# Alternating ScalarE's output copies with gate banks in slot 20 of a two-layer GLA and retention trunk

## The reference

```python
h = _rmsnorm(x, norm_w)
z = jnp.einsum('btd,dc->btc', h, w_in).astype(F32)
gq, gk, gv, gg, glr, rq, rk, rv, rg = _split_cols(z)
...
o_a = o_a * lax.rsqrt(jnp.mean(o_a * o_a, axis=-1, keepdims=True) + EPS) * gla_norm_w.astype(F32)
o_a = o_a.reshape(B, T, GLA_WIDTH) * jax.nn.silu(gg)
mu = jnp.mean(o_b, axis=-1, keepdims=True)
var = jnp.mean(jnp.square(o_b - mu), axis=-1, keepdims=True)
o_b = ((o_b - mu) * lax.rsqrt(var + GN_EPS)).reshape(B, T, RET_WIDTH)
o_b = (o_b * ret_norm_w.astype(F32) + ret_norm_b.astype(F32)) * jax.nn.silu(rg)
mixed = jnp.concatenate([o_a, o_b], axis=-1).astype(x.dtype)
y = x + jnp.einsum('btc,cd->btd', mixed, w_out)
```

## Time and profile before

| | us |
|---|---|
| median of 3 runs | 1630.08 |
| lowest, highest | 1627.74, 1633.01 |
| the profiled execution's own time | 1630.65 |
| its span (first to last instruction) | 1628.8 |
| PE busy | 1598.0 (98%) |
| DVE busy | 1116.3 (69%) |
| ACT busy | 641.2 (39%) |
| POOL busy | 839.1 (52%) |
| mean granted TensorE clock | 0.996 of full |

### The profile page before, as it was taken

One profiled execution on the slowest core, in us unless ns is written; L12 is line 12 of the kernel. 1 busy time (PEld: TensorE's weight loads), 2 busy tenths in 40 slices (PEclk: granted clock), 3 DMA queues, 4 the chain that ended last, 5 costly groups with the idle time before them and its releaser, 6 DMA issues.

```text
span 1628.8 us, 30453 instructions
## 1 busy us (share of the span) xinstructions
PE 1598.0 (98%) x11840; PEld 1303.4 (80%) x11840; DVE 1116.3 (69%) x2402; ACT 641.2 (39%) x1184; POOL 839.1 (52%) x646
## 2 busy tenths in 40 slices
PE   9998999989999999999999999999999999999998
PEld 7787878878888887888778888787788887878887
DVE  5955876768765585557855477758887567784684
ACT  5423434334343443434443344343433435343342
POOL 4543645646455464455544455456544455554465
PEclk9999999999999999999999999999999999999999
DMA  8356656766445564466643676576764466553654
GB/s 287 114 97 166 200 202 162 215 180 207 173 118 156 168 197 137 122 169 154 203 136 100 160 162 191 162 194 188 184 189 134 126 166 163 173 170 92 168 160 144
DMA packets 389296, 268.32 MB, mean 165 GB/s; under 512 B 290720, under 2 KB 293280, under 8 KB 389152
## 3 DMA queue, kind: packets, MB, share of 16 engines
q1 hardware_dynamic: 315280, 131.86, 31.8%
q10 hardware_dynamic: 73872, 134.51, 26.1%
HBM read 219.21 MB, written 47.07 MB: 163 GB/s over the span
## 4 chain that ended last, share of the span: by engine, by line
PE 78%; DVE 11%; DMA 4%; SPq 3%; issue 2%; ACT 1%; POOL 0%; ACTq 0%; POOLq 0%; DVEq 0%
PE bank L785 70%; DVE region L1582 3%; PE bank L1032 2%; PE bank L994 2%; PE bank L1043 1%; SPq L486 1%; DMA out_o_rows<-region 1%; SPq L472 1%; DVE bns L1559 1%; DVE tmp L1599 1%; PE bank L751 1%; PE bank L1017 1%; DVE m_lo L1615 1%; PE bank L879 1%; DMA out_k_rows<-region 1%
## 5 line engine op out<-in xcount | busy, mean ns | idle before, releaser
L283 POOL TENSOR_TENSOR w_lo<-w_stage,w_hi 128x512 fp32r<-128x512 f32 x344 | 480.5, 1417 | 430.9 <-ACT w_hi L276 430.1
L785 PE MATMUL bank<-h_hi,w_hi 128*128 128x512 f32 x1016 | 406.7, 400 | 5.3 <-DVE region L1588 3.7
L785 PE MATMUL bank<-h_lo,w_hi 128*128 128x512 f32 x1016 | 398.2, 392 | 0.0
L785 PE MATMUL bank<-h_hi,w_lo 128*128 128x512 f32 x1016 | 396.8, 391 | 0.0
L276 ACT ACTIVATE w_hi<-w_stage 128x512 fp32r<-128x512 f32 x344 | 199.8, 624 | 477.6 <-PE bank L785 402.3
L283 POOL TENSOR_TENSOR w_lo<-ss,w_hi 128x512 fp32r<-128x512 f32 x112 | 150.1, 1359 | 173.2 <-ACT w_hi L276 173.0
L785 PEld LDWEIGHTS bank<-h_hi,w_hi 128*128 128x128 f32 x1016 | 191.4, 188 | 59.8 <-issue 18.9
L785 PEld LDWEIGHTS bank<-h_hi,w_lo 128*128 128x128 f32 x1016 | 191.4, 188 | 41.4
L785 PEld LDWEIGHTS bank<-h_lo,w_hi 128*128 128x128 f32 x1016 | 191.6, 189 | 37.2
L785 PE MATMUL bank<-w_hi,m_hi 128*128 128x512 f32 (+1 forms) x520 | 202.0, 388 | 6.7 <-DVE region L1588 6.1
L785 PE MATMUL bank<-w_lo,m_hi 128*128 128x512 f32 (+1 forms) x520 | 200.8, 386 | 0.0
(11 more groups left out here) (233 smaller groups left out, 2256.3 us busy)
## 6 DMA issues: line engine op xcount, KB each, us to landing
w_stage<-in_w_slots ACTq DMA_DIRECT2D x344, 256.0 KB, 3.7
ss<-in_w_slots ACTq DMA_DIRECT2D x112, 256.0 KB, 4.1
region<-in_x_prompt SPq DMA_DIRECT2D x32, 512.0 KB, 6.0
out_o_rows<-region SPq DMA_DIRECT2D x64, 256.0 KB, 3.2
v_b<-in_w_slots ACTq DMA_DIRECT2D x56, 256.0 KB, 3.0
region<-out_o_rows SPq DMA_DIRECT2D x192, 64.0 KB, 3.0
out_k_rows<-region SPq DMA_DIRECT2D x32, 256.0 KB, 3.3
k_n<-out_k_rows SPq DMA_DIRECT2D x256, 32.0 KB, 2.9
```

What stands on the lines that cost most here:

```text
L283: pool.tensor_tensor(w_lo[:, r, c], stage(h), w_hi[:, r, c].bitcast(f32), ALU.subtract).then_inc(lo_done, 1)
L785: i = pe.matmul(dst, x, y, start=(s == 0 and kk == 0 and c == 0), stop=(s == 3 and kk == 1 and c == 2), skip_group_check=True)
```

## The change

ACT's copies of output pairs 0 and 1 for g = 1 and its four tanh of the first gate used to run as pair 0, pair 1, tanh of banks 0 to 3, the tanh at the head of slot 21. Now slot 20 runs pair 0, tanh of banks 0 and 1, pair 1, tanh of banks 2 and 3. DVE's slot 20 ran stats of tile 0 and of tile 1, and slot 21 began with the four silu. Now slot 20 runs silu of banks 0 and 1, stats of tile 0, silu of banks 2 and 3, stats of tile 1. In block 0 each pair's `first_gates` stand in front of its silu, in slot 20 and in slot 25 (there two banks and their silu, then the other two). DVE's four `turned(0, h)` move from the end of slot 18 to the end of slot 19, behind `states(1, 1)`. No operation is added or removed. The diff, cut to its core:

```diff
+                    def outputs_out(g, j):
+
+                        act.wait_ge(o_ps.sem, o_ps.at(n, 4 * g + 2 * j + 2))
...
+                    def gates_out(g, j):
+
+                        if j == 0 and g == 1:
+                            act.wait_ge(mix_sb.sem, mix_sb.at(n, 4))
+                        elif j == 0 and kind == 1:
+                            act.wait_ge(s_v.sem, s_v.at(l, V_SS[1]))
+                        for q in (2 * j, 2 * j + 1):
+                            if n > 0:
+                                wait_bank(act, n, 4 + g, q)
+                            else:
+                                act.wait_ge(first_g, 4 * g + q + 1)
+                            nc.scalar.activation(g_t[:, q, :], P[q][:, :], ACT.Tanh, scale=0.5).then_inc(g_tanh.sem, 1)
...
-                        if w in (21, 25):
...
+                        for j in (0, 1) if w == 25 else ():
+                            gates_out(1, j)
...
                         for j in (0, 1) if w in (12, 20) else ():
...
+                            outputs_out(w // 20, j)
+                            if w == 20:
+                                gates_out(0, j)
...
+                    def gates(g, j):
+
+                        if n == 0:
+                            first_gates(g, j)
+                        silu(g, j)
...
-                        if w in (21, 25):
-                            if n == 0:
-                                first_gates(w // 25)
-                            silu(w // 25)
+                        for j in (0, 1) if w == 25 else ():
+                            gates(1, j)
...
+                        if w == 19:
+                            for h in range(HEADS):
+                                turned(0, h)
                         if w in (12, 20):
-                            stats(g, 0)
-                            stats(g, 1)
+                            for j in range(2):
+                                if w == 20:
+                                    gates(0, j)
+                                stats(g, j)
...
-                        if w == 18:
-                            for h in range(HEADS):
-                                turned(0, h)
```

More of the change, by code:

```diff
@@ L1154, in sample_work @@
                                                      ACT.Tanh, scale=0.5).then_inc(tg_s.sem, 1)
+                    def outputs_out(g, j):
+                        act.wait_ge(o_ps.sem, o_ps.at(n, 4 * g + 2 * j + 2))
+                        o8 = o_n[:, 2 * j:2 * j + 2, :].rearrange("p t (i h n) -> p (t i) h n", i=2, h=2)
+                        nc.scalar.activation(o8[:, :, 0, :], OUT_TWO[j][0][:, :].rearrange("p (a n) -> p a n", a=4), ACT.Copy)
+                        for z in range(2):
+                            src, dst = slice(CH * (1 - z), CH * (1 - z) + CH), slice(CH * z, CH * z + CH)
+                            i = nc.scalar.activation(o8[dst, :, 1, :], OUT_TWO[j][1][src, :].rearrange("p (a n) -> p a n", a=4), ACT.Copy)
+                        i.then_inc(o_sb.sem, 2)
+                    def gates_out(g, j):
[9 more added lines that the diff above has]
+                            nc.scalar.activation(g_t[:, q, :], P[q][:, :], ACT.Tanh, scale=0.5).then_inc(g_tanh.sem, 1)
                     late = 2 * int(n == 0)
@@ L1583, in norm, with silu @@
                         i.then_inc(normed.sem, 1)
-                    def silu(g):
-                        for q in range(4):
+                    def silu(g, j):
+                        for q in (2 * j, 2 * j + 1):
                             vec.wait_ge(g_tanh.sem, g_tanh.at(n, 4 * g + q + 1))
@@ L1645, in first_exponents, with first_gates @@
                         vec.tensor_tensor(e4, e4, rb[:, :].unsqueeze(1).to_broadcast([128, 4, BLK]), ALU.mult).then_inc(first_ex, 1)
-                    def first_gates(g):
-                        for q in range(4):
+                    def first_gates(g, j):
+                        for q in (2 * j, 2 * j + 1):
                             wait_bank(vec, n, 4 + g, q)
```

7 lines of the change are left out of this document (removed).

## The result

The changed kernel takes 1643.26 us (median of 6 runs, 1640.14 to 1650.22) where the kernel before, in 6 runs beside it, takes 1631.67 (1627.74 to 1634.38). The ratio is 1.0079 with a 95% interval of 1.0062 to 1.0096: 0.8% slower.

What follows compares the result with a forecast made beforehand. DVE's queue of slots 20 to 24, not slot 21, was taken to set the end. 9.2 + 3.0 + 0.7 + 0.2 + 0.7 - 3.0 = +10.8 us on 1630.65 gave 1641.4, less 0.57, rounded 1641; range 1629.5 to 1647.

Steps and rivals of the forecast that it cites:

- blocks 2 and 7, slot 25: PE's wait for DVE's silu at the second gate grows from 0.30 to 2.6 us, 2.3 a block.
- blocks 3 and 6, slot 25: PE's wait for DVE's silu at the second gate grows from 2.61 to 4.9 us, 2.3 a block.
- blocks 3 and 6, clock behind it: After the 4.9 us waits at slot 25 PE's clock drops, costing 1.5 us each, 3.0 in all.
- block 4: DVE's queue runs 4.4 us later against 4.0 us of cover from sample matmuls: +0.7, between 0 and 2.
- block 5: Norm of tile 1 runs free before POOL's split, so the delay is only about 0.2 us.
- block 1: Slot 21 starts 4.1 us earlier, but a 3.7 us wait at L918 and a clock drop follow: +0.7, between -2 and +2.
- block 0: Outputs start 4.9 us earlier behind states; 2.4 of the queue's gain is left at slot 25: -3.0, between -4.9 and 0.
- The 2.3 of a block: Slots 20 to 25, worked out on block 2: later silu 3 0.28, tile 1's stats 1.60, root wait 0.4, delaying everything behind.
- The collisions: Block 2 norms against POOL's splits: tile 1 meets two and tile 3 four, as now, so no net change.
- The rival in which they are dodged: Slot 23's split_lo falls beside stats instead of norm, saving 2.1 us a block: 1629 to 1632, no difference; chance 0.17.
- The rule that I set aside: GpSimd/VectorE contention would hold tile 0's norm beside tile 1's root up to 1 us in four blocks, 4 us more.
- The collision step: Block 1: norm of tile 1 runs free, giving back 2.1 us; two more splits precede tile 3's norm, 1.05 each.

Runs made afterwards that it cites:

- dve_order_undone: The changed kernel with DVE's slot 20 order put back, stats of both tiles and then the four silu: 1633.72 us, ratio 0.9994 to the kernel before.
- stats_behind_silu: The kernel before with only DVE's stats of tile 1 moved behind the four silu of the first gate: 1648.53 us, ratio 1.0091 to the kernel before.
- turned_undone: The changed kernel with DVE's turned heads put back to slot 18, ahead of the second half of the states: 1650.62 us, ratio 1.0097 to the kernel before.
- turned_alone: The kernel before with only DVE's turned heads moved behind the second half of the states: 1631.33 us, ratio 0.9974 to the kernel before.
- transposes_later: The kernel before with turned heads behind states and DVE's four next-block transposes moved from slot 23 to 27: 1621.84 us, ratio 0.9930 to the kernel before.

## Why the prediction was right

It said 1641.0, slower, and the result is 1643.26, or 1.0079 times 1630, 1643. By its steps, forecast against the change in the account:

| step | forecast | measured |
|---|---|---|
| blocks 2 and 7, slot 25 | +2.3 each | +2.15 each |
| blocks 3 and 6, slot 25 | +2.3 each | +3.26, +4.28 |
| blocks 3 and 6, clock behind it | +1.5 each | +1.72, +2.15 |
| block 4 | +0.7 | +0.73 |
| block 5 | +0.2 | +0.08 |
| block 1 | +0.7 | -1.10 |
| block 0 | -3.0 | -3.43 |
| elsewhere | 0 | +2.3 |
| sum | +10.8 | +14.3 |

That the sum came out so near is in part luck. It was too low by 2.9 for m_lo in blocks 3 and 6, 0.9 for the clock there and 2.3 elsewhere, and too high by 1.8 in block 1 and 0.7 in blocks 0, 2 and 7.

**What bounds.** Right: DVE's queue between slot 20 and slot 25, not slot 21, sets the end. dve_order_undone and stats_behind_silu bear it out from both sides. Relieving slot 21 was worth nothing in blocks 2 to 7.

**The 2.3 of a block.** Right, and in its parts: norm starts 8.84 us behind PE's slot 20 in blocks 2 and 6 of after, where it was 6.98 and 7.05 (from PE's and DVE's timelines); forecast 8.8 and 7.0. Norm of tile 1 waits 0.34 for the root (forecast 0.4). The collisions do cancel as said: 0.87 + 2.96 for the eight norms against 3.76. The rival in which they are dodged fell: the split starts at 561.40, the norms at 561.47.

**The rule that I set aside.** Norm of tile 0 at 560.26 to 561.13 beside the root at 560.43 takes 0.87 for four, each as if alone. The row of before decided rightly. By the rule of the Trainium skill, GPSIMD Engine Reference, Specifications, read without exception, it would have been held up to 1 us. What is held in the stretches read here is held by the splits of 128x512 elements and by m_lo of the same size.

**Blocks 3 and 6: the term was mis-sized.** The step was that everything behind the norms moves with them by the same 2.3. It doesn't: POOL's splits near m_lo moved by less, and m_lo is held by 1.1 us more in block 3 and by 2.1 in block 6, where each half is caught. I had looked for collisions at the norms and not at the end of the same queue. That is 3.1 us, 2.9 after the 0.15 a block by which the rest came out below 2.3.

**The clock behind the waits.** Right in kind. The granted clock in the stretch around the end of block 3's wait at 780.49, after, with block 2 below it (windows: us, busy of PE, PE weight load, DVE, ACT, POOL, clock, DMA share, GB/s):

```profile
778.00:786.00 8.00, 5.51 (x14) 4.39 (x15) 8.00 (x13) 1.89 (x3) 2.88 (x2) 0.57 0.91 182
...
581.00:586.00 5.00, 4.59 (x20) 3.84 (x21) 4.63 (x8) 2.23 (x4) 3.32 (x3) 1.00 1.16 234
```

Behind 5.87 us of idle time PE's matmuls start 0.43 us apart and later 0.23, half the clock (1.2 GHz) and then the full one (2.4); ten of them at the lower one cost 2.0 us. Behind 2.45 in block 2 the clock is 1.00, as forecast. That this holds for every wait of this length was not to be had from one row, though: in turned_undone the clock falls behind 2.46 at the same place, and the stretch behind it is 1.6 us longer than before.

**Block 4** and **block 5** came as forecast. In block 4 the first silu of slot 25 starts 4.55 us later (forecast 4.4), against a cover of 4.0, though the parts differ: the norms of tile 3 take 5.05 instead of 3.01, and m_lo is free, 1.24 instead of 3.00.

**Block 1: the sign was wrong, the size within its bounds of -2 to 2.** The wait at slot 21 is gone, not 1 us, and L918 waits 2.46 instead of 3.7. The collision step held: the norms of tiles 0 and 1 run free and those of tiles 2 and 3 pay for it.

```profile
358.60 0.87 DVE L1590 TENSOR_SCALAR region<-region,rstd 128x128 f32<-128x128 f32 x4
359.80 0.88 DVE L1590 TENSOR_SCALAR region<-region,rstd 128x128 f32<-128x128 f32 x4 [0.34 <-POOL rstd L652]
```

These eight took 3.50 us before, and the eight of slot 22 take 5.87 in after and took 3.77: 2.1 more, as said. What failed is where the queue starts. The weights reach ACT earlier than in the trace of before: POOL's splits behind them run at 349.70 in after,

```profile
349.70 2.55 POOL L283 TENSOR_TENSOR w_lo<-ss,w_hi 128x512 fp32r<-128x512 f32 x2 [5.08 <-ACT w_hi L276]
```

right behind the outputs' end at 349.8, against 352.95 and 354.91, some 2 and 4 us behind it, before. So norm starts 8.8 us behind the outputs and not 10.9. I had taken the lateness of one trace for a property of the kernel; slot 21's wait in block 1 was 3.67, 0.39, 1.42, 3.33 and 1.24 in before, stats_behind_silu, dve_order_undone, turned_alone and transposes_later. Against that the clock did drop behind L918, where I had taken half.

**Block 0** came as forecast: L1032 without idle time, at 1.98 us, and slot 25 waiting 1.4 us longer (1.75 against 0.31) where I had put 1.3, the 4.9 won at the outputs less the 3.6 that I left of it.

**Elsewhere** I had nothing. 2.2 us lie ahead of slot 18 of block 0, in work that is the same in both: a wait "issue" of 2.19 where it was 1.37, and the clock behind a wait of 2.12 (below). turned_alone and turned_undone have such differences too, at other places, while medians of many runs don't show them; so I count them as what one profile differs from another, and not as the change's.

The total of the silu waits is 20.1 instead of some 16: 2.7 us more in blocks 2, 3, 6 and 7, which is m_lo, and 1.75 in block 0 and 0.65 in block 4 that I had left out of it, less the 1 us of block 1's slot 21.

## What to carry to other kernels

When an in-order engine sets the end some slots later, don't let a step that is already runnable queue behind one that waits for another engine's last product: the stats of tile 1 cost 2.05 us in blocks 2 and 7 that way, 1.6 of them their own, and with stats ahead of each pair's silu the same alternation cost 0.10. If you move a piece of one queue, look for what else it meets in the queues that don't move or move by less, down to the point where someone waits: here 0.1 us of delay brought 1.1 more. A split moved off large instructions held the next small one for 1.1 to 1.3 us. Don't price a wait for a transfer from a single trace. Work of the next block that stands ahead of that point is the first thing to move: with few lines it gave 0.4%, and 0.7% together with the turned heads.

## What the runs showed of the hardware

That the clock falls behind an idle time of 2.1 to 2.6 us is not settled by its length. PE's matmuls of L785 behind a wait of 2.12 us at 71 us in block 0 of after start 0.43 apart,

```profile
71.22 1.13 PE L994 MATMUL bank<-region,k_n 64*64 64x128 f32 x32 [2.12 <-DVE k_n L1512]
72.28 0.79 PE L785 MATMUL bank<-h_hi,w_hi 128*128 128x512 f32 x1
72.88 0.63 PE L785 MATMUL bank<-h_lo,w_hi 128*128 128x512 f32 x1
```

and in before, behind 2.11 us at the same place, 0.23 apart:

```profile
72.38 0.50 PE L785 MATMUL bank<-h_hi,w_hi 128*128 128x512 f32 x1
72.72 0.40 PE L785 MATMUL bank<-h_lo,w_hi 128*128 128x512 f32 x1
```

Eight matmuls take 3.16 instead of 1.74 us: 1.4 us. Behind the two waits of 2.46 for L918 in after the clock falls, and behind those of 2.45 and 2.46 at slot 25 it doesn't, while in turned_undone it falls behind 2.46 at slot 25 of block 2 and in stats_behind_silu behind 2.25; behind 2.61 at slot 25 of block 3 it is 1.00 in before, and in turned_alone, behind 2.60 at the same place, it falls for longer than anywhere else, for 13 matmuls:

```profile
774.73 0.76 PE L785 MATMUL bank<-w_hi,m_hi 128*128 128x512 f32 x1 [2.60 <-DVE region L1588]
775.29 0.63 PE L785 MATMUL bank<-w_lo,m_hi 128*128 128x512 f32 x1
775.72 0.63 PE L785 MATMUL bank<-w_hi,m_lo 128*128 128x512 f32 x1
```

That costs 2.8 us, the difference of the stretch behind it. What makes the clock fall at one of these waits and not at the other stays open. Behind the longer ones, from 3.8 to 7.3 us at slot 25, the stretch behind was 1.0 to 2.6 us longer in every kernel that had them. Over the whole span 41 matmuls of L785 start some 0.43 us after the one before them in after, and 12 in before: at 0.2 us each, about 6 us of the 14.3 are clock.
